# ScalarE's turn of an expert loop begun one split sooner, and fetched result rows added in eight operations of 512 columns

## The chip, the cores and the metric

The kernel runs on one core of a Trainium2 chip. The metric is the device time of one execution in microseconds. Five engines work side by side and wait for each other only through semaphores: TensorE (PE, matrix products into PSUM), VectorE (DVE), ScalarE (ACT), GpSimd (POOL) and SyncE (SP, which here issues the transfers).

## The reference

The kernel computes a two-layer encoder over 256 tokens of width 1024 in fp32. Layer 0 is Fourier mixing and a dense SwiGLU, layer 1 neighbourhood attention and a SwiGLU of 8 experts, of which each token takes two; a last RMSNorm closes it. The change lies in the experts:

```python
def moe_swiglu(h, w_router, b_router, w_gate, w_up, w_down):
    t = h.reshape(-1, D)                                  # 256 x 1024
    logits = t @ w_router + b_router                      # 8 experts
    top_val, top_idx = lax.top_k(logits, TOP_K)           # 2 of 8
    gates = jax.nn.softmax(top_val, axis=-1)
    ...
    def expert_block(args):                               # w_gate, w_up: 1024 x 3584
        xb, e = args                                      # w_down: 3584 x 1024
        return (jax.nn.silu(xb @ w_gate[e]) * (xb @ w_up[e])) @ w_down[e]
    ...
    out = jnp.zeros((T, D), h.dtype).at[tok_sorted].add(y * gate)
```

## The kernel before, in words

Products are done in fp32r, where one fp32 product takes three matmuls: each operand is split into a high part and a rest (the low part), and `three` (lines 1244 to 1250) adds high by high, high by low and low by high. All weights stream through the core once, in pieces of 128 x 2048 values (1 MB). For piece j there are three jobs: SP loads it into one of 7 buffers `raw`; ScalarE writes the high part (`split_hi`, line 454) into one of 3 buffers `w_hi`; VectorE writes the low part (`split_lo`, line 752) into one of 3 buffers `w_lo`; TensorE uses both with 12 matmuls of 512 columns. Since there are 3 buffers (`SPLIT = 3`), the split of piece j + 3 waits until TensorE has used piece j (`piece_used`).

An expert has 42 pieces, in the order of `EXPERT`: seven steps c of `gate c` (2 pieces), `up c` (2), and from step 1 on `down c-1` (2), and `down 6` at the end. After each gate ScalarE makes the silu (`silu`, line 672) and copies the transposed hidden values (line 678); after each up VectorE makes `hid` (line 1083).

Up to 128 tokens are given to each expert in a first sweep (experts 0 to 7); a second sweep for tokens beyond that is behind a test (`over`) and isn't entered with this input. Experts 0 to 6 are turns of a hardware loop on each engine (`Fori(0, LAST)`), expert 7 is written out behind it. TensorE does the first gate of the next expert (its pieces 0 and 1) at the end of its turn. ScalarE and VectorE run `AHEAD = SPLIT + 1 = 4` pieces ahead at the boundary: their turns skip j = 0 and end with the split of the next expert's piece 3. Inside a turn, at place j, the operations of that place come first and then the split of piece j + 3:

```python
for j, (kind, c, half) in enumerate(EXPERT):
    if j < AHEAD - SPLIT:
        continue
    if (kind, half) == ("gate", 1):
        silu(E, c)
...
    if ahead or j + SPLIT < PER_EXPERT:
        split_hi(j + SPLIT, E)
```

So ScalarE's turn begins with the silu of step 0, which waits until pieces 0 and 1 are used. The program builder sets an activation table load (ACT_TABLE_LOAD) in front of the first activation of a piece of program that needs another table than the one that may be in place; in the loop's body that is now the silu (line 672).

Results of experts 0 to 6 are written to a table in HBM (`results`), one row for each slot. While expert 7 runs, POOL fetches for each token its first and second row into `hn_hi` and `hn_lo` (line 435), and VectorE adds them to `h`, times the gates `g1` and `g2`, in `add_terms(0)` and `add_terms(1)`, which stand behind `hid` of steps 2 and 3 and ahead of the split of that place. `gate_weights` (six small operations) stands in step 1. Expert 7's own result is added at the end (`add_result`, line 1116).

Of the kernel before, what the change touches and what calls it, by code (L numbers as in the profile page):

```python
# [26 lines left out]
P = 128  # L27
D = 1024
S = 256
NB = S // P  # L30
# [11 lines left out]
BANK = 512  # L42
PIECE = 2048
RAW = 7
SPLIT = 3
# [64 lines left out]
PER_EXPERT = len(EXPERT)  # L110
assert PER_EXPERT % RAW == 0 and PER_EXPERT % SPLIT == 0

AHEAD = SPLIT + 1
# [12 lines left out]
def trunk(nc, x, norm_mix, norm_ffn, w_in, w_out, w_qkv, w_o, ffg, ffu, ffd, router_w, router_b,  # L126
          ewg, ewu, ewd, final_norm, gains_c, slide_c, dft_c, mask_c, ident_c, before_c, count_c, out):
    f32, f32r, bf16, i32, u32 = mybir.dt.float32, mybir.dt.float32r, mybir.dt.bfloat16, mybir.dt.int32, mybir.dt.uint32
    ALU, ACT, AX = mybir.AluOpType, mybir.ActivationFunctionType, mybir.AxisListType
# [22 lines left out]
    h = sb("h", [P, NB, D])  # L152
# [9 lines left out]
    half_power = sb("half_power", [P, NB])  # L162
# [37 lines left out]
             ("most", [P, 1], f32), ("flag", [P, 1], i32), ("rstd_of_slot", [P, 1], f32)]  # L200
    at_home("pad_arena")
    arena_start = nc.sbuf_base
    mo_more = [("y_row", [P, D], f32), ("place", [P, 2, NB], f32), ("past", [P, 2, NB], f32), ("source", [P, 2, NB], u32)]
    moe_l += mo_more
    sizes = [sum(width_of(shape) for _, shape, _ in l) for l in (fourier_l, attn_l, moe_l, bias_l + bias_l)]
    sb("arena", [P, max(sizes) // 4])
# [3 lines left out]
    fo, mo = (layout(l, arena_start) for l in (fourier_l, moe_l))  # L210
# [23 lines left out]
    def sem(name):  # L234
# [36 lines left out]
    y_act, y_dve, s_result, places_made, s_terms, terms_added, s_no_result = (sem(n) for n in (  # L271
        "y_act", "y_dve", "s_result", "places_made", "s_terms", "terms_added", "s_no_result"))
# [18 lines left out]
    SECOND = (NE, 2 * NE)  # L291
# [153 lines left out]
    def _(act):  # L445
        made = [0]

        def split_hi(j, E):
            s, w = slot_of(j, E, RAW), slot_of(j, E, SPLIT)
            rounds = 16 * (j // RAW + 1) if E is None else 16 * ((N0 + j) // RAW + 1) + E * (16 * PER_EXPERT // RAW)  # L450
            act.wait_ge(raw_in[s], rounds)
            if has_before(j, E, SPLIT):
                act.wait_ge(piece_used, piece(j, E, SPLIT))
            nc.scalar.activation(w_hi[w][:], raw[s][:], ACT.Copy).then_inc(hi_made, 1)  # L454
# [125 lines left out]
        n = at["down"][-1][-1]  # L580
# [112 lines left out]

        def expert(E, ahead, kept=True):

            for j, (kind, c, half) in enumerate(EXPERT):
                if j < AHEAD - SPLIT:
                    continue
                if (kind, half) == ("gate", 1):
                    silu(E, c)  # L700
                    if c:
                        hidden_hi(E, c - 1)
                if (kind, c, half) == ("down", STEPS - 2, 0):
                    if ahead:
                        gather_hi(E + 2)
                    hidden_hi(E, STEPS - 1)
                if (kind, c, half) == ("down", STEPS - 1, 1):
                    (result_hi if kept else result_copy)(E)
                if ahead or j + SPLIT < PER_EXPERT:
                    split_hi(j + SPLIT, E)  # L710
            if ahead:
                for j in range(PER_EXPERT + SPLIT, PER_EXPERT + AHEAD):
                    split_hi(j, E)

        gather_hi(1)
        assert made[0] == N1
        for j in range(SPLIT, AHEAD):
            split_hi(j, 0)
        with act.Fori(0, LAST) as E:
            expert(E, True, False)  # L720
        act.wait_ge(flag_done, 1)
# [2 lines left out]
        with act.If(over):  # L724
            act.wait_ge(e_gather, 2)
            act.wait_ge(hn_made, NB)
            act.wait_ge(terms_added, 2 * NB)
            for b in range(NB):
                nc.scalar.activation(mo["hn_hi"][:, b], hn[:, b], ACT.Copy).then_inc(hnr_hi, 1)
            gather_hi(NE + 1)  # L730
            for j in range(PER_EXPERT, PER_EXPERT + AHEAD):
                split_hi(j, LAST)
            with act.Fori(*SECOND) as E:
                expert(E, True)
            act.wait_ge(e_added, NB * (NE + 1))
        squares(4)

    @block.vector
    def _(dve):
# [108 lines left out]
        n = at["w_out"][0][-1]  # L848
# [24 lines left out]
        for c in range(DC):  # L873
# [5 lines left out]
            for b in range(NB):  # L879
                dve.wait_ge(d_silu, NB * c + b + 1)  # L880
                projected(dve, d_up, c, at["up"][c], b)
                if c:
                    dve.wait_ge(d_hidT, NB * (c - 1) + b + 1)
                nc.vector.scalar_tensor_tensor(out=hid[b][:, :w], in0=U[b][:, :w], scalar=rstd[:, 1, b:b + 1],
                                               in1=silu_g[b][:, :w], op0=ALU.mult, op1=ALU.mult).then_inc(d_hid, 1)
# [5 lines left out]
        n = at["down"][-1][-1]  # L891
# [52 lines left out]
        for p in range(PAIRS):  # L944
            for i in (2 * p, 2 * p + 1):
                dve.wait_ge(a_score, i + 1)
                if i >= 2:
                    dve.wait_ge(a_exp, NB * (i - 1))
                nc.vector.scalar_tensor_tensor(out=silu_g[i % 2][:].rearrange("p (n k) -> p n k", n=NB), in0=two(G[i % 2]),
                                               scalar=float(HD) ** -0.5, in1=head_bias(i), op0=ALU.mult, op1=ALU.add).then_inc(a_biased, 1)  # L950
# [41 lines left out]
        for b in range(NB):  # L992
            dve.wait_ge(sq_half, b + 1)
            half = h[:, b, BANK:]
            nc.vector.tensor_tensor_reduce(out=mo["xg"][:, BANK * b:BANK * (b + 1)], in0=half, in1=half, scale=1.0,
                                           scalar=mo["sumsq_half"][:, b:b + 1], op0=ALU.mult, op1=ALU.add,
# [13 lines left out]
        for b in range(NB):  # L1010
            nc.vector.scalar_tensor_tensor(out=mo["rest"][:, b], in0=G[b][:, NE:2 * NE], scalar=rstd[:, 3, b:b + 1],
                                           in1=mo["rb"][:], op0=ALU.mult, op1=ALU.add).then_inc(low_added, 1)
        for b in range(NB):
            dve.wait_ge(low_added, b + 1)
            link(nc.vector.scalar_tensor_tensor(out=mo["logit"][:, b], in0=G[b][:, 0:NE], scalar=rstd[:, 3, b:b + 1],
                                                in1=mo["rest"][:, b], op0=ALU.mult, op1=ALU.add))
        for n, (src, one) in enumerate((("logit", "first"), ("rest", "second"))):
# [6 lines left out]
            if n == 0:  # L1024
                link(nc.vector.scalar_tensor_tensor(out=mo["rest"][:], in0=mo["first"][:], scalar=-3e38,
                                                    in1=mo["logit"][:], op0=ALU.mult, op1=ALU.add))
# [11 lines left out]
        def gather_copy(E1):  # L1038

            for q in range(2):  # L1040
                cs = slice(BANK * q, BANK * (q + 1))
                dve.wait_ge(e_gather, 2 * by_products(E1) - 1 + q)
                if isinstance(E1, int) and E1 == 1:
                    made_copy = nc.vector.tensor_tensor(mo["xg"][:, cs], (G, U)[q][1][:], mo["gain"][:, 0, cs], ALU.mult)
                else:
                    made_copy = nc.vector.tensor_copy(mo["xg"][:, cs], (G, U)[q][1][:])
                made_copy.then_inc(e_xg[q], 1)
# [60 lines left out]

        def add_result(E, e):
            for b in range(NB):  # L1110
                dve.wait_ge(terms_added, NB + b + 1)
                for q in range(2):
                    dve.wait_ge(e_scatter, NB * (2 * (E - LAST) + q) + b + 1)
                    part = h[:, b, BANK * q:BANK * (q + 1)]
                    src = T[q] if b == 0 else (G, U)[q][1]
                    last = nc.vector.scalar_tensor_tensor(out=part, in0=src[:], scalar=mo["weight"][:, b, bass.ds(e, 1)],
                                                          in1=part, op0=ALU.mult, op1=ALU.add)
                last.then_inc(e_added, 1)
# [19 lines left out]
            link(nc.vector.tensor_tensor(mo["second"][:], mo["second"][:], each_token(mo["g2"][:]), ALU.mult))  # L1138
            link(nc.vector.tensor_tensor(mo["weight"][:], mo["first"][:], mo["second"][:], ALU.add))

        def add_terms(n):

            for b in range(NB):
                dve.wait_ge(s_terms, 16 * 2 * NB)
                if n:
                    dve.wait_ge(terms_added, b + 1)
                nc.vector.scalar_tensor_tensor(out=h[:, b], in0=mo[("hn_hi", "hn_lo")[n]][:, b].bitcast(f32),
                                               scalar=mo[("g1", "g2")[n]][:, b:b + 1], in1=h[:, b],
                                               op0=ALU.mult, op1=ALU.add).then_inc(terms_added, 1)

        def expert(E, sweep, ahead, kept=True):

            e = E - NE if sweep else E
# [3 lines that stand above are left out]
                if (kind, half) == ("gate", 1) and c:  # L1157
                    hidden_rest(E, c - 1)
                if (kind, c, half) == ("gate", 1, 1) and ahead and not sweep:
                    row_numbers(E)  # L1160
                if (kind, half) == ("up", 1):
                    hidden(E, c)
                    if c == 0 and kept:
                        next_selection(E, e, sweep, ahead)
                    elif c == 0:
                        dve.wait_ge(e_token, E)
                        select(sweep, e + 1)
                    if not kept or sweep:
                        pass
                    elif c == 1:  # L1170
                        gate_weights()
                    elif c == 2:
                        add_terms(0)
                    elif c == 3:
                        add_terms(1)
                    if c == STEPS - 1 and ahead and sweep:
                        gather_copy(E + 2)
                if (kind, c, half) == ("down", STEPS - 2, 0):
                    if ahead:
                        gather_lo(E + 2)  # L1180
                        rstd_is_one(E)
                    hidden_rest(E, STEPS - 1)
                if (kind, c, half) == ("down", STEPS - 1, 1):
                    (result_rest if kept else result_copy)(E)
                if ahead or j + SPLIT < PER_EXPERT:
                    split_lo(j + SPLIT, E)
            if ahead:
                for j in range(PER_EXPERT + SPLIT, PER_EXPERT + AHEAD):
                    split_lo(j, E)
            if kept:  # L1190
                add_result(E, e)
# [38 lines left out]
        for b in range(NB):  # L1230
            dve.wait_ge(fin_rstd, b + 1)
            for q in range(2):
                cs = slice(BANK * q, BANK * (q + 1))
# [594 lines left out]
```

## Time and profile before

| | |
|---|---|
| median of 3 runs | 1378.86 us (1378.75 to 1379.13) |
| the profiled execution: time | 1379.58 us |
| its span | 1377.8 us |
| TensorE busy | 1349.4 us (98%) |
| VectorE busy | 1111.5 us (81%) |
| ScalarE busy | 920.1 us (67%) |
| GpSimd busy | 33.8 us (2%) |
| granted TensorE clock, mean | 0.993 of full speed |

The span is the time from the first to the last instruction of the profiled execution; its time is a little longer. Busy time of an engine counts its own operations, not waits. In rows of a timeline the columns are: start in us from the span's start, duration in us, engine, line, operation, tile written <- tiles read, shape, count; then in brackets the idle time of the engine before it and what ended it. A count of x2 or x3 means operations merged into one row, whose duration runs from the first start to the last end. An engine's operations may overlap by about 0.1 us, since one begins before the last one's end is recorded. The duration of a matmul is modelled: matmuls start about every 0.23 us and are shown as 0.39 us long, so the starts say more than the durations.

### The profile page before, as it was taken

Reading aid. Unit: us, or ns where it says so; the run is one execution under the profiler, and the core shown is the slowest. Engines: PE = TensorE matmul, PEld = TensorE weight load, DVE = VectorE, ACT = ScalarE, POOL = GpSimd, SP = SyncE. Lnnn points to the kernel's source line nnn. Section 1 sums busy time; section 2 is a strip of 40 time slices with the busy share of each in tenths; the row PEclk is TensorE's granted clock in tenths of the full one; section 3 lists DMA queues with packets and bytes.
Section 4 is the critical chain, followed back from the end, with each engine's and each line's share of the span. In section 5 each row is a group of like instructions: output and inputs, shape, how many; then the busy total and the mean of one; then the engine's idle time right before and its main releaser. Section 6 shows DMA issues by size and latency. Waiting matters only on the chain.

```text
span 1377.8 us, 17441 instructions
## 1 busy us (share of the span) xinstructions
PE 1349.4 (98%) x6369; PEld 1120.4 (81%) x6369; DVE 1111.5 (81%) x811; ACT 920.1 (67%) x747; POOL 33.8 (2%) x48
## 2 busy tenths in 40 slices
PE   9999999999999999999999999999999999999997
PEld 7888888787877887888788788888878888888775
DVE  5756666655678888888988888898888889889987
ACT  6554444445647777777777777777777777777674
POOL 0000000000110000000000000000000000002000
PEclk9999999999989999999999999999999999999999
DMA  9666775462339999999999999999999999999992
GB/s 347 218 206 181 216 214 191 163 204 92 113 125 372 374 378 362 394 372 364 392 372 370 369 391 372 370 383 366 384 367 392 369 368 388 373 377 381 394 362 93
DMA packets 194940, 431.27 MB, mean 313 GB/s; under 512 B 19601, under 2 KB 22033, under 8 KB 194897
## 3 DMA queue, kind: packets, MB, share of 16 engines
q1 hardware_dynamic: 178752, 415.66, 82.8%
q0 software_dynamic: 3360, 11.78, 2.2%
q10 hardware_dynamic: 12784, 3.26, 1.7%
q8 instruction: 27, 0.44, 0.1%
q14 instruction: 17, 0.13, 0.0%
HBM read 424.89 MB, written 5.78 MB: 313 GB/s over the span
## 4 chain that ended last, share of the span: by engine, by line
PE 89%; DVE 5%; ACT 3%; issue 2%; DMA 0%; ACTq 0%; POOL 0%; DVEq 0%
PE bank_G L1248 10%; PE bank_G L1250 10%; PE bank_G L1249 10%; PE bank_U L1248 9%; PE bank_U L1250 9%; PE bank_U L1249 9%; PE bank_Y L1248 8%; PE bank_Y L1250 8%; PE bank_Y L1249 8%; DVE w_lo L752 2%; PE bank_T L1689 2%; ACT w_hi L454 1%; PE bank_T L1248 1%; PE bank_T L1250 1%; PE bank_T L1249 1%
## 5 line engine op out<-in xcount | busy, mean ns | idle before, releaser
L752 DVE TENSOR_TENSOR w_lo<-raw,w_hi 128x2048 fp32r<-128x2048 f32 x390 | 885.8, 2289 | 195.2 <-ACT w_hi L454 195.1
L454 ACT ACTIVATE w_hi<-raw 128x2048 fp32r<-128x2048 f32 x390 | 747.0, 1919 | 286.7 <-PE bank_U L1250 91.1
L1248 PE MATMUL bank_Y<-w_hi,hidT_hi 128*128 128x512 f32 x492 | 192.3, 391 | 0.0
L1250 PE MATMUL bank_Y<-w_hi,hidT_lo 128*128 128x512 f32 x492 | 191.6, 390 | 0.0
L1249 PE MATMUL bank_Y<-w_lo,hidT_hi 128*128 128x512 f32 x492 | 191.5, 389 | 0.0
L1248 PE MATMUL bank_G<-w_hi,xg_hi 128*128 128x512 f32 x448 | 175.6, 392 | 11.0 <-DVE w_lo L752 10.0
L1248 PE MATMUL bank_U<-w_hi,xg_hi 128*128 128x512 f32 x448 | 179.1, 400 | 0.0
L1250 PE MATMUL bank_U<-w_hi,xg_lo 128*128 128x512 f32 x448 | 175.0, 391 | 0.0
L1250 PE MATMUL bank_G<-w_hi,xg_lo 128*128 128x512 f32 x448 | 174.5, 390 | 0.0
L1249 PE MATMUL bank_U<-w_lo,xg_hi 128*128 128x512 f32 x448 | 174.5, 390 | 0.0
L1249 PE MATMUL bank_G<-w_lo,xg_hi 128*128 128x512 f32 x448 | 174.4, 389 | 0.0
L1248 PEld LDWEIGHTS bank_G<-w_hi,xg_hi 128*128 128x128 f32 x448 | 84.1, 188 | 32.5 <-DVE w_lo L752 9.3
L1250 PEld LDWEIGHTS bank_Y<-w_hi,hidT_lo 128*128 128x128 f32 x492 | 92.3, 188 | 19.3
L1248 PEld LDWEIGHTS bank_Y<-w_hi,hidT_hi 128*128 128x128 f32 x492 | 92.3, 188 | 19.3
L1249 PEld LDWEIGHTS bank_Y<-w_lo,hidT_hi 128*128 128x128 f32 x492 | 92.4, 188 | 18.8
L1250 PEld LDWEIGHTS bank_U<-w_hi,xg_lo 128*128 128x128 f32 x448 | 84.1, 188 | 18.3
L1250 PEld LDWEIGHTS bank_G<-w_hi,xg_lo 128*128 128x128 f32 x448 | 84.1, 188 | 17.6
L1249 PEld LDWEIGHTS bank_G<-w_lo,xg_hi 128*128 128x128 f32 x448 | 84.1, 188 | 17.1
L1249 PEld LDWEIGHTS bank_U<-w_lo,xg_hi 128*128 128x128 f32 x448 | 84.3, 188 | 16.2
L1248 PEld LDWEIGHTS bank_U<-w_hi,xg_hi 128*128 128x128 f32 x448 | 84.2, 188 | 15.9
L1248 PE MATMUL bank_G<-w_hi,act_hi 128*128 128x512 f32 (+1 forms) x176 | 67.6, 384 | 2.2 <-DVE act_lo L777 1.4
L1248 PE MATMUL bank_U<-w_hi,act_hi 128*128 128x512 f32 (+1 forms) x176 | 67.6, 384 | 0.3 <-DVE act_lo L773 0.3
(302 smaller groups left out, 1366.6 us busy)
## 6 DMA issues: line engine op xcount, KB each, us to landing
raw<-in_expert_w_gate SPq DMA_DIRECT2D x112, 1024.0 KB, 7.4
raw<-in_expert_w_up SPq DMA_DIRECT2D x112, 1024.0 KB, 7.5
raw<-in_expert_w_down SPq DMA_DIRECT2D x112, 1024.0 KB, 7.4
raw<-in_nat_w_qkv SPq DMA_DIRECT2D x12, 1024.0 KB, 5.1
raw<-in_ffn_w_gate SPq DMA_DIRECT2D x11, 1024.0 KB, 8.9
raw<-in_ffn_w_up SPq DMA_DIRECT2D x11, 1024.0 KB, 6.0
raw<-in_ffn_w_down SPq DMA_DIRECT2D x11, 1024.0 KB, 5.1
raw<-in_fourier_w_out SPq DMA_DIRECT2D x4, 1024.0 KB, 15.9
```

Source lines behind the costliest of these rows:

```text
L454: nc.scalar.activation(w_hi[w][:], raw[s][:], ACT.Copy).then_inc(hi_made, 1)
L752: nc.vector.tensor_tensor(w_lo[w][:], raw[s][:], w_hi[w][:].bitcast(f32), ALU.subtract).then_inc(lo_made, 1)
L1248: nc.tensor.matmul(out_, xh, wh, start=start, stop=False)
L1249: nc.tensor.matmul(out_, xh, wl, start=False, stop=False)
L1250: return nc.tensor.matmul(out_, xl, wh, start=False, stop=stop)
L1689: last = nc.tensor.transpose(T[c % 2][:, P * k:P * (k + 1)], hid[c % 2][:, P * k:P * (k + 1)], ident[:])
```

## The change

ScalarE's turn now begins at j = 0, with the split of piece 3, and ends with the split of piece 2 of the next expert; what stood before the loop for piece 3 goes. In front of each turn stands a silu of one column of `half_power` (a constant) into a new one-column tile, which nobody reads. VectorE's and SP's turns stay as they are. `add_terms(n)`, two operations of 1024 columns for each n, becomes `add_term(n, b, q)`, one operation of 512 columns; eight of them stand in steps 2 to 5 of expert 7, one behind `hid` (q = 0) and one ahead of the split of the first down piece (q = 1) of each step. The count that `add_result` and the second sweep wait for becomes 4 x NB = 8.

```diff
-... ("source", [P, 2, NB], u32)]
+... ("source", [P, 2, NB], u32), ("silu_first", [P, 1], f32)]
@@ ScalarE
         def expert(E, ahead, kept=True):
 
+            nc.scalar.activation(mo["silu_first"][:], half_power[:, 0:1], ACT.Silu)
             for j, (kind, c, half) in enumerate(EXPERT):
-                if j < AHEAD - SPLIT:
-                    continue
                 if (kind, half) == ("gate", 1):
                     silu(E, c)
...
                 if ahead or j + SPLIT < PER_EXPERT:
                     split_hi(j + SPLIT, E)
-            if ahead:
-                for j in range(PER_EXPERT + SPLIT, PER_EXPERT + AHEAD):
-                    split_hi(j, E)
 
         gather_hi(1)
         assert made[0] == N1
-        for j in range(SPLIT, AHEAD):
-            split_hi(j, 0)
         with act.Fori(0, LAST) as E:
             expert(E, True, False)
@@ VectorE
         def add_result(E, e):
             for b in range(NB):
-                dve.wait_ge(terms_added, NB + b + 1)
+                dve.wait_ge(terms_added, 4 * NB)
...
-        def add_terms(n):
-
-            for b in range(NB):
-                dve.wait_ge(s_terms, 16 * 2 * NB)
-                if n:
-                    dve.wait_ge(terms_added, b + 1)
-                nc.vector.scalar_tensor_tensor(out=h[:, b], in0=mo[("hn_hi", "hn_lo")[n]][:, b].bitcast(f32),
-                                               scalar=mo[("g1", "g2")[n]][:, b:b + 1], in1=h[:, b],
-                                               op0=ALU.mult, op1=ALU.add).then_inc(terms_added, 1)
+        def add_term(n, b, q):
+
+            cs = slice(BANK * q, BANK * (q + 1))
+            dve.wait_ge(s_terms, 16 * 2 * NB)
+            if n:
+                dve.wait_ge(terms_added, 2 * b + q + 1)
+            nc.vector.scalar_tensor_tensor(out=h[:, b, cs], in0=mo[("hn_hi", "hn_lo")[n]][:, b, cs].bitcast(f32),
+                                           scalar=mo[("g1", "g2")[n]][:, b:b + 1], in1=h[:, b, cs],
+                                           op0=ALU.mult, op1=ALU.add).then_inc(terms_added, 1)
...
-                    elif c == 2:
-                        add_terms(0)
-                    elif c == 3:
-                        add_terms(1)
+                    elif 2 <= c < 6:
+                        add_term((c - 2) // 2, c % 2, 0)
...
+                if (kind, half) == ("down", 0) and kept and not sweep and 1 <= c < 5:
+                    add_term((c - 1) // 2, (c - 1) % 2, 1)
```

## Rows read from the trace of the kernel before

**Rows 1.** The page's chain that ended last, by engine.
```profile
PE 89%; DVE 5%; ACT 3%; issue 2%; DMA 0%; ACTq 0%; POOL 0%; DVEq 0%
```

**Rows 2.** Waits of TensorE, 410 to 1250 us, then 1250 to 1378: total, times, longest.
```profile
PE bank_G L1248 <- DVE w_lo L752: 6.4, 7, 0.9
...
PE bank_G L1248 <- DVE w_lo L752: 3.6, 3, 1.6
```

**Rows 3.** Timeline of ScalarE at one boundary; last, all table loads of line 672.
```profile
525.05 1.93 ACT L454 ACTIVATE w_hi<-raw 128x2048 fp32r<-128x2048 f32 x1 [0.31 <-PE bank_Y L1250]
527.77 1.93 ACT L454 ACTIVATE w_hi<-raw 128x2048 fp32r<-128x2048 f32 x1 [0.80 <-PE bank_G L1250]
530.63 1.28 ACT L672 ACT_TABLE_LOAD   x1 [0.93 <-PE bank_G L1250]
531.92 0.69 ACT L672 ACTIVATE silu_g<-bank_G,rstd_of_slot 128x512 f32<-128x512 f32 x1
532.51 5.51 ACT L454 ACTIVATE w_hi<-raw 128x2048 fp32r<-128x2048 f32 x3
...
L672 ACT ACT_TABLE_LOAD x7: 1283/1283/1283, 410.7 to 1130.3; - x7
```

**Rows 4.** Timeline of VectorE at the same boundary.
```profile
529.73 2.29 DVE L752 TENSOR_TENSOR w_lo<-raw,w_hi 128x2048 fp32r<-128x2048 f32 x1 [0.35 <-ACT w_hi L454]
534.45 4.49 DVE L752 TENSOR_TENSOR w_lo<-raw,w_hi 128x2048 fp32r<-128x2048 f32 x2 [2.43 <-ACT w_hi L454]
```

**Rows 5.** Timeline of TensorE at the same boundary.
```profile
530.06 0.39 PE L1250 MATMUL bank_G<-w_hi,xg_lo 128*128 128x512 f32 x1
...
535.50 0.39 PE L1250 MATMUL bank_U<-w_hi,xg_lo 128*128 128x512 f32 x1
536.79 0.50 PE L1248 MATMUL bank_G<-w_hi,xg_hi 128*128 128x512 f32 x1 [0.90 <-DVE w_lo L752]
...
537.61 0.40 PE L1248 MATMUL bank_G<-w_hi,xg_hi 128*128 128x512 f32 x1
```

**Rows 6.** Timeline of ScalarE at the last boundary, behind the loop.
```profile
1247.28 1.92 ACT L454 ACTIVATE w_hi<-raw 128x2048 fp32r<-128x2048 f32 x1 [0.80 <-PE bank_G L1250]
1250.00 0.69 ACT L672 ACTIVATE silu_g<-bank_G,rstd_of_slot 128x512 f32<-128x512 f32 x1 [0.80 <-PE bank_G L1250]
```

**Rows 7.** Timeline of ScalarE in the dense layer and at the kernel's start.
```profile
79.59 1.92 ACT L454 ACTIVATE w_hi<-raw 128x2048 fp32r<-128x2048 f32 x1 [1.12 <-POOL rstd L398]
81.53 1.28 ACT L572 ACT_TABLE_LOAD   x1
82.82 1.27 ACT L572 ACTIVATE silu_g<-bank_G,rstd 128x512 f32<-128x512 f32 x2
...
3.47 0.20 ACT L506 ACTIVATE silu_g<-half_power 128x2 f32<-128x2 f32 x1
```

**Rows 8.** Timeline of VectorE in the last expert, steps 2 and 4.
```profile
1286.08 0.74 DVE L1083 SCALAR_TENSOR_TENSOR hid<-bank_U,rstd_of_slot,silu_g 128x512 f32<-128x512 f32 x1
1286.74 2.47 DVE L1147 SCALAR_TENSOR_TENSOR h<-hn_hi,g,h 128x1024 f32<-128x1024 f32 x2
1289.13 6.69 DVE L752 TENSOR_TENSOR w_lo<-raw,w_hi 128x2048 fp32r<-128x2048 f32 x3
...
1324.04 2.28 DVE L752 TENSOR_TENSOR w_lo<-raw,w_hi 128x2048 fp32r<-128x2048 f32 x1
1326.60 2.29 DVE L752 TENSOR_TENSOR w_lo<-raw,w_hi 128x2048 fp32r<-128x2048 f32 x1 [0.28 <-ACT w_hi L454]
```

**Rows 9.** Timeline of TensorE in the last expert, steps 2 and 4.
```profile
1289.59 0.39 PE L1250 MATMUL bank_Y<-w_hi,hidT_lo 128*128 128x512 f32 x1
1291.57 0.47 PE L1248 MATMUL bank_G<-w_hi,xg_hi 128*128 128x512 f32 x1 [1.59 <-DVE w_lo L752]
...
1292.33 0.39 PE L1248 MATMUL bank_G<-w_hi,xg_hi 128*128 128x512 f32 x1
...
1327.11 0.39 PE L1248 MATMUL bank_G<-w_hi,xg_hi 128*128 128x512 f32 x1
```

More of the change, by code:

```diff
@@ L202, in trunk @@
     arena_start = nc.sbuf_base
-    mo_more = [("y_row", [P, D], f32), ("place", [P, 2, NB], f32), ("past", [P, 2, NB], f32), ("source", [P, 2, NB], u32)]
+    mo_more = [("y_row", [P, D], f32), ("place", [P, 2, NB], f32), ("past", [P, 2, NB], f32), ("source", [P, 2, NB], u32), ("silu_first", [P, 1], f32)]
     moe_l += mo_more
@@ L726, in _ @@
             act.wait_ge(hn_made, NB)
-            act.wait_ge(terms_added, 2 * NB)
+            act.wait_ge(terms_added, 4 * NB)
             for b in range(NB):
@@ L730, in _ @@
             gather_hi(NE + 1)
-            for j in range(PER_EXPERT, PER_EXPERT + AHEAD):
+            for j in range(PER_EXPERT, PER_EXPERT + SPLIT):
                 split_hi(j, LAST)
@@ L734, in _ @@
                 expert(E, True)
+            split_hi(PER_EXPERT + SPLIT, SECOND[1] - 1)
             act.wait_ge(e_added, NB * (NE + 1))
```

## The prediction

> **What bounds the kernel now.** I read the page's chain first: nine tenths of it is TensorE [rows 1], so only an edit that takes away time in which TensorE stands still, or adds some, can move the end. The views of waits say where it stands still while the experts run. In the loop over experts 0 to 6 there are seven waits, all for a low part (`w_lo`) that VectorE makes, and in the last expert three, up to 1.6 us long [rows 2]. The reader should then go to the timelines of one boundary between experts and of the last expert, since the change edits just these two places.
>
> At the boundary, TensorE finishes the second gate piece of the new expert (piece 1) at U = 530.06 + 0.39 = 530.45. It goes on with pieces 2 and 3 without a gap, and stands before piece 4: 535.50 to 537.61 is 2.11 us for four starts that take 4 x 0.227 elsewhere ((535.50 - 530.06) / 24 = 0.227), so 1.20 us are lost [rows 5]. Why is piece 4 late? ScalarE had piece 3's high part done at 527.77 + 1.92 = 529.69, waited for U, and only then loaded its activation table (1.28 us), made the silu, and began piece 4's high part at 532.51 [rows 3]. VectorE took that up at 534.45 after 2.43 us of idleness [rows 4], ended at 534.45 + 2.29 = 536.74, and TensorE started at 536.79. The table load happens seven times, once at the head of each turn [rows 3]. The eighth boundary, where the loop has ended, has no table load: the silu begins 0.80 us after the split before it [rows 6], and no wait of TensorE stands there. Seven boundaries lose 7 x 1.20 = 8.4 us.
>
> In the last expert the two long stalls come from `add_terms`. Two 1024-column additions hold VectorE for 1289.13 - 1286.74 = 2.39 us ahead of a low part [rows 8]; it ends at 1289.13 + 2.29 = 1291.42, and TensorE goes on at 1291.57. From 1289.59 to 1292.33 are 2.74 us for four starts, so 2.74 - 0.91 = 1.83 us lost [rows 9]. The three waits have 3.6 us with 1.6 as the longest [rows 2], so two of that size, together 3.66 us lost; the third, 3.6 - 2 x 1.6 = 0.4 us, follows `gate_weights` and isn't touched.
>
> **The turn of ScalarE.** The edit removes no work from the turn; it puts the loop's head one split sooner and a one-column silu in front, so the table load belongs to that silu, which waits for no semaphore. New order: split of piece 2, loop branch, table load, one-column silu, split of piece 3, (wait for U) silu, split of piece 4. SP's and POOL's queues and VectorE's order stay; no DMA is moved.
>
> Step by step, in the times of this boundary. The split of piece 2 ends at 525.05 + 1.92 = 526.97. A table load that waits for nothing starts 0.02 us after the operation before it and the next silu follows at once: 79.59 + 1.92 = 81.51, then 81.53, then 82.82 [rows 7]. So: load at 526.99, one-column silu at 528.28. The nearest row for it is a two-column copy of 0.20 us [rows 7], and one operation may begin 0.10 before the last one's end (531.92 + 0.69 against 532.51 [rows 3]), so the split of piece 3 begins between 528.38 and 528.48. I take 528.43, 0.66 later than now (527.77).
>
> Does that hurt? Its high part ends at 530.35, 0.10 before U, so the silu starts right after U. The low part of piece 3 moves from 529.73 to 530.39 and ends at 532.68. Piece 3's first slot on TensorE is at 535.73 - 12 x 0.227 = 533.01. A low part must be ready some time before its slot: the one that ended at 536.74 cost 1.20 us, so for the slot at 535.73 the latest harmless end is 535.54, 0.19 ahead. For piece 3 that is 532.82; now it ends at 532.02. Slack left 0.14 us: it fits, barely.
>
> And piece 4: silu at U + 0.04 = 530.49 in place of 531.92, so all behind it is 1.43 us earlier; the low part ends at 536.74 - 1.43 = 535.31, before 535.54. Slack 0.23 us, and the stall goes: -1.20 us, seven times, **-8.4 us**. At the first boundary the load falls into the idleness before piece 0 is used up; at the eighth the one-column silu (0.1 to 0.2 us) fits into the 0.80 us of idleness [rows 6]. Cover that costs nothing now: if the split of piece 3 came later than 528.43 by more than 0.14 us, each further us is a us lost per boundary, up to the 1.2 gained.
>
> The branch itself has no row. It was hidden so far: it lay between the issue of the split at 527.77 and U, at most 2.68 us. Now only the split of piece 2 (1.92 us) covers it, so from 0 to 0.76 us of it can be exposed. I take 0: the first boundary has no branch back, yet the seven waits come to 6.4 us with 0.9 as the longest [rows 2], so it waits as long as the others.
>
> A switch of tables could cost more than its load. The row has 81.51 to 82.82, 1.31 us, for a complete switch with work on both sides [rows 7], and the sum goes by that. The Trainium skill, "ScalarE: Activation LUTs", section "What ACT_TABLE_LOAD costs", puts a switch at the load and a drain beside it, about 2.66 us together. That speaks against the change: by the row the boundary gains 1.20, by the page next to nothing (the rival of the drain, below). The trace doesn't agree with the page here.
>
> **The fetched rows.** Four 1024-column additions become eight of 512 columns. A 1024-column one takes 1.20 us in sequence (2.39 / 2). A 512-column one has no row: below it is half, 0.60; above, if the price went by the instruction, 1.20. VectorE's three-operand operation on 512 columns (`hid`, the same form, one input in PSUM) takes 0.66 in sequence: it starts at 1286.08, the next operation at 1286.74 [rows 8]. I take 0.66. VectorE's work grows by 8 x 0.66 - 4 x 1.20 = 0.5 us; what counts is where it stands.
>
> In an undisturbed step the low part of the next gate's first piece runs 1324.04 to 1326.33 [rows 8] and its slot is 1327.11 [rows 9]. From the stall, the margin ahead of a slot is 1291.42 against 1289.82 (the slot) + 1.83: an end of 1289.59 is harmless, so 0.23. Slack: 1327.11 - 0.23 - 1326.33 = 0.55 us (check: 2.39 - 0.55 = 1.84 lost, as measured). One addition of 0.66 gives 0.11 us lost. The next low part (1326.60, ending 1328.89, slot 1329.83) has slack 0.71. In the changed kernel it starts at 1324.70 + 2.21 (a low part in sequence) + 0.66 (the second addition) = 1327.57, ends at 1329.86, and may end at 1329.60 + 0.11 already lost: 0.15 more. Low parts follow each other at 2.21 and pieces at 12 x 0.227 = 2.72, so VectorE regains 0.5 us with each of the next pieces, and nothing is carried into the next step. Four steps (c = 2 to 5) lose 4 x 0.26 = 1.0 us in place of 3.66: **-2.6 us**. With 0.60 per addition it is 4 x 0.14 = 0.6, so -3.1; with 1.20 it is 4 x (0.65 + 0.69) = 5.4, so +1.7. The rows were fetched by then: the first addition follows `hid` without idleness [rows 8], so the waits in front of the additions pass. `add_result` waits for eight in place of four, long done.
>
> **Sum.** -8.4 - 2.6 = -11.0 us. The profiled execution has a span of 1377.8 and a time of 1379.58, 1.8 around it; changed, the span is 1366.8. The median of the runs is 1378.86, 0.7 below the profiled time; I take the difference off the median: **1367.9 us**.
>
> **Rivals.**
> *The branch back is exposed.* Then the split of piece 3 is later than now by 0.66 + 0.76 = 1.42, and its low part ends at 532.02 + 1.42 = 533.44 against 532.82: 0.62 lost. The silu then waits for ScalarE (531.11), low part 4 ends at 535.93, within 535.54 + 0.62: no more. The six boundaries behind a branch give 6 x 0.62 = 3.7 back: 1371.6. For it: nothing shows the branch alone. Against: TensorE's own branch at 530.3 leaves no gap. Chance 0.12. The Trainium skill ("Runtime: NRT & Kernel Launch", section "Instruction fetch mechanics") says that a taken branch whose target has left the instruction window waits for a fetch; no row here shows such a wait.
>
> *The engine drains at a switch.* If a switch cost as much again as its load (1.28 us more), the split of piece 3 would be 1.94 us later than now, its low part would end at 533.96 and 1.14 be lost, against 1.20 now: 6 x 0.06 = 0.4 gained, with the first boundary's 1.2 (its load is under cover) and the additions' 2.6 together 4.2: 1374.7. Against: the 1.31 us of [rows 7]. Chance 0.04. With the drain of the Trainium skill's page named above, 1.24 us would be lost at each of the six, and the time be 1375.3.
>
> *The additions are dear.* At 1.20 each the second part costs 1.7 in place of giving 2.6: 1372.2. Against: the row of `hid`. Chance 0.05.
>
> *Slower.* The branch back has no cover at all: ScalarE takes it only when the split of piece 2 has ended. Its whole length is bounded by 2.68 us, from the issue of the split at 527.77 to U [rows 3, 5]. Split of piece 3 later by 0.66 + 2.68 = 3.34, less the 0.80 that its low part has now (532.82 - 532.02): 2.54 lost, 1.34 more than now, over six boundaries +8.0, less 1.2 (the first) and 2.6: +4.2, 1383.1. It decides from some 2.0 us exposed. Against: a branch taken only behind a split had 0.76 us in the trace (529.69 to U), not 2.68. Chance 0.02.
>
> *The change does nothing at the boundary:* a load stays before the waited silu, or another wait lies just behind (a transfer of weights). Then only -2.6: 1376.3. Against: in the seven boundaries ScalarE is released by TensorE [rows 3], and the two lists of TensorE's waits name no transfer [rows 2]; the one-column silu is the body's first operation. Chance 0.05.
>
> **How the numbers follow.** My forecast has 0.72, with its own range from 1366.3 (additions at 0.60 take 0.5 us off 1367.9, no loss from them at all another 0.6, and half a us for what the steps round) to 1369.8 (0.3 us left at each of six boundaries). The range 1366.2 to 1372.0 takes in the exposed branch and leaves out the four last rivals, 0.16. About 0.2% (2.8 us) is what a measurement of this kernel can tell from no change. Faster by more: 0.72 + 0.12 + 0.04 + 0.05 = 0.93; within: no effect at the boundary, 0.05; slower: 0.02.
>
> **What would show it.** In the changed trace: the table load about 0.02 us behind the split of piece 2 and at no other place; the split of piece 3 some 0.66 us later relative to U; the silu 0.04 us after U; the seven waits of TensorE gone from the loop; silus of one boundary to the next 118.7 us apart in place of 119.9. In the last expert the waits of 1.6 us gone and up to eight of 0.1 to 0.2 us in their place, in steps 2 to 5; an addition of about 0.74 us. The prediction is wrong if the load isn't followed at once by the one-column silu, if the split of piece 3 starts over 0.8 us late, or if a wait for piece 3 appears on TensorE.

## The result

The changed kernel takes 1367.91 us (median of 4 runs, 1367.32 to 1367.96) against 1378.80 us (4 runs, 1378.04 to 1379.13) for the kernel before. The ratio is 0.9921 with an interval from 0.9904 to 0.9938: faster by 10.9 us, where 11.0 were forecast. The span of the profiled execution went from 1377.8 to 1366.0 us, 11.8 less, of which 0.6 lie ahead of the experts: TensorE ends the first gate of expert 0 at 410.54 before and at 409.97 now. From there to the end it is 967.2 against 956.0 us, 11.2 less.

### The profile page after: what moved, and what is told of

Read it like the earlier page. It is cut to its first block, busy times and chain, and to the rows that moved or that the text cites. A ratio compares the mean times of both kernels' runs of the same rounds, so it can differ in the third digit from the quotient of the medians.

```text
span 1366.0 us, 17462 instructions
## 1 busy us (share of the span) xinstructions
PE 1347.7 (99%) x6369; PEld 1120.3 (82%) x6369; DVE 1111.9 (81%) x815; ACT 922.8 (68%) x755; POOL 33.3 (2%) x48
## 4 chain that ended last, share of the span: by engine, by line
PE 93%; DVE 3%; ACT 1%; DMA 1%; SPq 1%; issue 1%; POOL 0%; DVEq 0%; ACTq 0%
PE bank_G L1243 10%; PE bank_G L1245 10%; PE bank_G L1244 10%; PE bank_U L1243 10%; PE bank_U L1245 10%; PE bank_U L1244 10%; PE bank_Y L1243 8%; PE bank_Y L1245 8%; PE bank_Y L1244 8%; PE bank_T L1684 2%; DMA raw<-in_fourier_w_out 1%; PE bank_T L1243 1%; PE bank_T L1245 1%; PE bank_T L1244 1%; DVE w_lo L747 1%
```

## The profile after

In the page, the parts that answer to [rows 1] and to the busy line: TensorE works 1347.7 us (1349.4 before), of a span 11.8 shorter, and the chain has 93% TensorE in place of 89%.

```profile
PE 1347.7 (99%) x6369; PEld 1120.3 (82%) x6369; DVE 1111.9 (81%) x815; ACT 922.8 (68%) x755; POOL 33.3 (2%) x48
...
PE 93%; DVE 3%; ACT 1%; DMA 1%; SPq 1%; issue 1%; POOL 0%; DVEq 0%; ACTq 0%
```

The waits of TensorE, 405 to 1245 us, are an empty list now. From 1240 us to the end one of the three of [rows 2] is left, that of `gate_weights`:

```profile
PE bank_G L1243 <- DVE w_lo L747: 0.4, 1, 0.4
```

ScalarE at the boundary of [rows 3] (columns as there):

```profile
523.31 1.92 ACT L454 ACTIVATE w_hi<-raw 128x2048 fp32r<-128x2048 f32 x1 [0.32 <-PE bank_Y L1245]
525.25 1.28 ACT L696 ACT_TABLE_LOAD   x1
526.54 0.20 ACT L696 ACTIVATE silu_first<-half_power 128x1 f32<-128x1 f32 x1
526.65 1.90 ACT L454 ACTIVATE w_hi<-raw 128x2048 fp32r<-128x2048 f32 x1
528.91 0.69 ACT L672 ACTIVATE silu_g<-bank_G,rstd_of_slot 128x512 f32<-128x512 f32 x1 [0.35 <-PE bank_G L1245]
```

The split of piece 2 ends at 523.31 + 1.92 = 525.23; the load starts 0.02 us later, branch included. The one-column silu takes 0.20 us and holds the next operation 0.11.

VectorE at the same boundary, the rows that answer to [rows 4]:

```profile
528.59 2.29 DVE L747 TENSOR_TENSOR w_lo<-raw,w_hi 128x2048 fp32r<-128x2048 f32 x1 [0.96 <-ACT w_hi L454]
531.43 4.49 DVE L747 TENSOR_TENSOR w_lo<-raw,w_hi 128x2048 fp32r<-128x2048 f32 x2 [0.55 <-ACT w_hi L454]
```

And TensorE, the rows that answer to [rows 5]: end of piece 1, first start of piece 2, last start of piece 3, first of piece 4.

```profile
528.33 0.39 PE L1245 MATMUL bank_G<-w_hi,xg_lo 128*128 128x512 f32 x1
528.55 0.39 PE L1243 MATMUL bank_U<-w_hi,xg_hi 128*128 128x512 f32 x1
...
533.76 0.40 PE L1245 MATMUL bank_U<-w_hi,xg_lo 128*128 128x512 f32 x1
534.00 0.40 PE L1243 MATMUL bank_G<-w_hi,xg_hi 128*128 128x512 f32 x1
```

U is 528.33 + 0.39 = 528.72 here. Between 533.76 and 534.00 are 0.24 us, a plain spacing, where 1.29 stood before [rows 5]. VectorE's idleness ahead of piece 4 has gone from 2.43 to 0.55.

In the last expert, VectorE in step 2, for [rows 8]:

```profile
1277.16 0.74 DVE L1078 SCALAR_TENSOR_TENSOR hid<-bank_U,rstd_of_slot,silu_g 128x512 f32<-128x512 f32 x1
1277.82 0.74 DVE L1142 SCALAR_TENSOR_TENSOR h<-hn_hi,g,h 128x512 f32<-128x512 f32 x1
1278.48 2.28 DVE L747 TENSOR_TENSOR w_lo<-raw,w_hi 128x2048 fp32r<-128x2048 f32 x1
1280.68 0.75 DVE L1142 SCALAR_TENSOR_TENSOR h<-hn_hi,g,h 128x512 f32<-128x512 f32 x1
1281.35 6.87 DVE L747 TENSOR_TENSOR w_lo<-raw,w_hi 128x2048 fp32r<-128x2048 f32 x3
...
1294.18 0.74 DVE L1078 SCALAR_TENSOR_TENSOR hid<-bank_U,rstd_of_slot,silu_g 128x512 f32<-128x512 f32 x1
```

An addition of 512 columns holds VectorE for 1278.48 - 1277.82 = 0.66 us. The step lasts 1294.18 - 1277.16 = 17.02 us. An undisturbed one lasted 16.80 before (`hid` at 1323.38 and 1340.18), so 0.22 us are lost. All four steps with additions, from `hid` at 1277.16 to `hid` at 1345.20, last 68.04 us, 0.84 more than four undisturbed ones.

## The experiments

Ten kernels, told in the order of the questions. A turn is the distance of two boundaries' silus (line 672) in ScalarE's timeline, from the second boundary to the seventh, by five. The last column is the time from U of the first boundary (where TensorE ends piece 1 of expert 0) to the end of the profiled execution. Both are finer measures than the time, since they leave out everything ahead of the experts, where the profiled executions of these kernels differ by up to 2.2 us in code that they share (U between 408.3 and 410.5). They are read from one execution each. The intervals of the ratios are 2.5 to 4.7 us wide, so kernels that lie 1 or 2 us apart can't be told apart by their times alone.

| kernel | time, us | ratio to before, interval | turn, us | first U to the end, us |
|---|---|---|---|---|
| before | 1378.8 | | 119.93 | 967.2 |
| changed | 1367.91 | 0.9904 to 0.9938 | 118.72 | 956.0 |
| turn_only | 1370.54 | 0.9926 to 0.9953 | 118.73 | 958.9 |
| terms_only | 1375.80 | 0.9968 to 0.9986 | 119.96 | 964.5 |
| no_silu | 1375.35 | 0.9964 to 0.9984 | 119.90 | 964.2 |
| silu_before_loop | 1370.51 | 0.9927 to 0.9954 | 118.72 | 959.2 |
| silu_in_front | 1372.48 | 0.9948 to 0.9975 | 119.05 | 961.6 |
| silu_512 | 1368.79 | 0.9916 to 0.9948 | 118.92 | 957.1 |
| silu_1024 | 1371.46 | 0.9935 to 0.9966 | 119.38 | 960.0 |
| one_1024_each_step | 1369.21 | 0.9918 to 0.9946 | 118.73 | 958.0 |
| additions_at_down | 1365.74 | 0.9891 to 0.9922 | 118.74 | 954.5 |
| load_before_loop_and_down | 1367.00 | 0.9899 to 0.9926 | 118.76 | 955.1 |

The turn of the kernel before is that of its seven table loads, (1130.3 - 410.7) / 6 [rows 3]. The kernel before was run again beside each group of kernels (medians 1378.57 to 1378.87 us), and each ratio is taken to its own.

**Each part alone.** `turn_only` has the changed ScalarE and the old `add_terms`; `terms_only` the old ScalarE and the eight additions.

> Only ScalarE's turn is changed; the additions are the four of 1024 columns as before. If the two parts are independent and the table load is the whole of the seven stalls, TensorE loses 1.20 us less at each of seven boundaries: 8.4 us less than before, 1370.4 us, with the two waits of 1.6 us still in the last expert. The rival, that the additions and the turn help each other (a lighter VectorE at the boundary), would leave it above 1371.5.

> Only the additions are changed; ScalarE's turn is as before. Steps 2 to 5 of the last expert are then each 17.01 us as in the changed kernel, 0.21 longer than an undisturbed one of 16.80, in place of two that lose 1.83: 3.66 - 0.85 = 2.8 us less than before, 1376.0 us, and the seven waits of 0.9 us stay. The rival, that the additions give nothing and the turn gives all of the 10.9 us, has 1378.8.

-8.3 us and -3.1 us against 1378.87 (the runs of the kernel before beside them), together -11.4 where both give -10.9. By the last column it is -8.3, -2.7 and -11.2. TensorE's waits, `turn_only` in the last expert, then `terms_only` in the loop:

```profile
PE bank_G L1243 <- DVE w_lo L747: 3.6, 3, 1.6
```
```profile
PE bank_G L1248 <- DVE w_lo L752: 6.4, 7, 0.9
```

Each part takes away its own waits and leaves the other's untouched; they are independent to 0.2 us, and the rivals of both expectations fall.

**Is it the sooner turn or the place of the load?** `no_silu` is the changed kernel without the new silu:

```diff
         def expert(E, ahead, kept=True):
-            nc.scalar.activation(mo["silu_first"][:], half_power[:, 0:1], ACT.Silu)
             for j, (kind, c, half) in enumerate(EXPERT):
```

> The changed kernel without the one-column silu: the turn begins one split sooner, but the program builder now sets two table loads into each turn, one in front of the split of piece 3 and one in front of the real silu, which waits for the gate. Theory (what counts is that no table load lies behind the wait for the gate): the first load is under cover (the split of piece 3 is 0.5 us later, within 0.8 of slack), the second costs what it cost before, 1.20 us at each of seven boundaries: 1367.9 + 8.4 = 1376.3 us. Rival (the sooner turn itself is what helps): 1367.9 to 1369 us.

1375.35 us, 7.4 above the changed kernel (8.4 expected): the time of `terms_only`. In the last column it is 8.2 above, and a turn is 1.18 longer, so 0.8 of the missing 1.0 lies outside the experts and isn't a smaller stall. ScalarE at its boundary:

```profile
524.78 1.28 ACT L454 ACT_TABLE_LOAD   x1
526.08 1.92 ACT L454 ACTIVATE w_hi<-raw 128x2048 fp32r<-128x2048 f32 x1
528.42 1.28 ACT L672 ACT_TABLE_LOAD   x1 [0.42 <-PE bank_G L1244]
529.72 0.69 ACT L672 ACTIVATE silu_g<-bank_G,rstd_of_slot 128x512 f32<-128x512 f32 x1
```

There are two loads now, since the copy of the split comes first in the body and is given a load of its own. The first costs nothing (the turn is that of `terms_only` to 0.06 us); the second stands behind the wait for the gate, and all seven waits are back (6.3 us in total). The sooner turn by itself gives nothing.

**And the load without the sooner turn?** `silu_before_loop` is the kernel before with one line, ahead of the loop and not in it:

```diff
+        nc.scalar.activation(mo["silu_first"][:], half_power[:, 0:1], ACT.Silu)
         with act.Fori(0, LAST) as E:
             expert(E, True, False)
```

> The kernel before with one single one-column silu ahead of the loop and nothing else changed (turns of ScalarE as before, old additions). The program builder then sets one table load ahead of the loop and none in it. If the load alone made the stalls, each boundary looks like the eighth of the kernel before, TensorE doesn't wait there, and the time is 8.4 us less than before: 1370.4 us, the same as with ScalarE's turn changed alone. Rival (the late start of the turn, at the wait for the gate, costs something by itself): between 1371 and 1378.

1370.51 us and a turn of 118.72, where `turn_only` has 1370.54 and 118.73. Both ways into the loop's body now leave the same table in place, and the builder sets no load into it. The boundary, without a load:

```profile
522.68 1.92 ACT L454 ACTIVATE w_hi<-raw 128x2048 fp32r<-128x2048 f32 x1 [0.32 <-PE bank_Y L1251]
525.40 1.92 ACT L454 ACTIVATE w_hi<-raw 128x2048 fp32r<-128x2048 f32 x1 [0.80 <-PE bank_G L1251]
528.27 0.69 ACT L672 ACTIVATE silu_g<-bank_G,rstd_of_slot 128x512 f32<-128x512 f32 x1 [0.96 <-PE bank_G L1251]
```

So the load behind the wait is the cause of the stall in the turns, and the late start of the turn costs nothing. The first boundary is an exception that the expectation didn't see. The one load stands behind the split of piece 3, the small silu behind it, and the real silu starts 0.73 us behind U (409.58 against 408.46 + 0.39). TensorE's first start of piece 4 is then 0.53 us behind the last of piece 3 (413.90 to 414.43) in place of 0.23. By the last column this kernel is 0.3 us behind `turn_only`.

**A load half under cover.** `silu_in_front` puts the one-column silu in front of the old turn, behind the split of piece 3:

```diff
         def expert(E, ahead, kept=True):
+            nc.scalar.activation(mo["silu_first"][:], half_power[:, 0:1], ACT.Silu)
             for j, (kind, c, half) in enumerate(EXPERT):
                 if j < AHEAD - SPLIT:
                     continue
```

> The kernel before with the one-column silu in front of each turn, the turn itself still begun with the wait for the gate. The table load (1.28 us) then starts when the split of piece 3 has ended (0.76 us before U), not at U: it ends 0.52 behind U, the small silu takes 0.10 to 0.20, the real silu starts 0.65 to 0.7 behind U in place of 1.47, so the split of piece 4 is 0.82 earlier and 0.38 of the 1.20 us is left at each of seven boundaries: 1378.8 - 5.7 = 1373.1 us. Rival (the load isn't started before the real silu is free to go): 1378.8 us.

1372.48 us; the turn of 119.05 leaves 119.05 - 118.72 = 0.33 us of stall (0.38 expected). The load starts when the split ends, and its last half microsecond sticks out past U, which is TensorE's start at 527.33 + 0.39 = 527.72:

```profile
525.03 1.92 ACT L454 ACTIVATE w_hi<-raw 128x2048 fp32r<-128x2048 f32 x1 [0.80 <-PE bank_G L1251]
526.97 1.28 ACT L696 ACT_TABLE_LOAD   x1
528.26 0.20 ACT L696 ACTIVATE silu_first<-half_power 128x1 f32<-128x1 f32 x1
528.37 0.67 ACT L672 ACTIVATE silu_g<-bank_G,rstd_of_slot 128x512 f32<-128x512 f32 x1
```

**How thin is the slack of piece 3?** The prediction had 0.14 us. Two kernels delay the split of piece 3 by a known amount, with a wider first silu (512 columns as fp32; 1024 as bf16 in the same room):

```diff
-            nc.scalar.activation(mo["silu_first"][:], half_power[:, 0:1], ACT.Silu)
+            nc.scalar.activation(mo["silu_first"][:], half_power[:, 0:1].to_broadcast([P, 512]), ACT.Silu)
```

> The changed kernel with the first silu 512 columns wide in place of one (its input is the same constant read again and again). It takes about 0.63 us in place of 0.20, so the split of piece 3 is 0.43 us later. From the changed kernel's trace the low part of piece 3 ends at 530.88 and its slot is at 531.27, with 0.19 of margin ahead of it: slack 0.20 us. So 0.23 lost at each of six boundaries (at the first the silu is under cover), 1.4 us: 1369.3 us, with six short waits of TensorE for piece 3. Rival (the slack isn't that thin, VectorE or the three buffers carry more): 1367.9 us.

> The changed kernel with the first silu 1024 columns wide (written as bf16, which halves the room and not the time): about 1.06 us in place of 0.20, the split of piece 3 0.86 us later. Beyond the slack of 0.20 that is 0.66 at each of six boundaries, 4.0 us: 1371.9 us. The real silu is then late as well, by 0.5 us, but piece 4 has by then as much more time as piece 3 has lost, so it doesn't add. If it added, 1374 to 1375. Rival (slack not thin): 1367.9 to 1369.

The silus take 0.63 and 1.05 us and the turns are 118.92 and 119.38: 0.20 and 0.66 lost, where 0.23 and 0.66 were expected. The times are 0.9 and 3.6 above the changed kernel's (1.4 and 4.0 expected); by the last column it is 1.1 and 4.0. At 512 columns the list of TensorE's waits is empty, where six short ones were expected; the loss shows in the starts at piece 3 alone (530.17, 530.48, 530.82, so 0.31 and 0.34 apart in place of 0.23). At 1024 columns TensorE waits six times, and for `bank_U`, that is for piece 3, no longer for piece 4:

```profile
PE bank_U L1246 <- DVE w_lo L750: 2.1, 6, 0.4
```

The delay of 0.86 beyond a slack of 0.20 is lost one for one, and the late silu doesn't add to it. The first boundary isn't among the six, since there the load and the silu lie in front of the first gate.

**Size or number of the additions?** `one_1024_each_step` leaves the four additions whole and puts one in each step:

```diff
                     elif 2 <= c < 6:
-                        add_term((c - 2) // 2, c % 2, 0)
+                        add_term((c - 2) // 2, c % 2)
...
-                if (kind, half) == ("down", 0) and kept and not sweep and 1 <= c < 5:
-                    add_term((c - 1) // 2, (c - 1) % 2, 1)
```

> The changed kernel's turn, and the four additions of 1024 columns left whole, but one in each of the steps 2 to 5, behind hid. VectorE is held 1.20 us against 0.55 of slack: 0.65 lost in each of four steps, 2.6 us, against 0.21 x 4 = 0.85 in the changed kernel and 3.66 with two in a step: 1369.7 us. Rival (what helps is the size of the operation, not how many stand in a step): 1370.7 us, as with the turn alone.

1369.21 us (1369.7 expected), and four waits of 0.39 us where two additions at once cost 1.6; the fifth of the list is that of `gate_weights`. The list, then VectorE:

```profile
PE bank_G L1240 <- DVE w_lo L747: 2.0, 5, 0.4
...
1277.18 0.74 DVE L1078 SCALAR_TENSOR_TENSOR hid<-bank_U,rstd_of_slot,silu_g 128x512 f32<-128x512 f32 x1
1277.84 1.27 DVE L1141 SCALAR_TENSOR_TENSOR h<-hn_hi,g,h 128x1024 f32<-128x1024 f32 x1
1279.03 6.69 DVE L747 TENSOR_TENSOR w_lo<-raw,w_hi 128x2048 fp32r<-128x2048 f32 x3
...
1294.66 0.75 DVE L1078 SCALAR_TENSOR_TENSOR hid<-bank_U,rstd_of_slot,silu_g 128x512 f32<-128x512 f32 x1
```

The step is 1294.66 - 1277.18 = 17.48 us, 0.68 lost, 2.7 in four steps. So each step has one allowance of 0.55 us behind `hid`, and what counts is how often it is used. Spreading over four steps brings about 1.0 of the 2.8 us. The other 1.8 come from halving the operations and putting the second halves one place later; which of the two it is was not tried apart.

**A better place.** `additions_at_down` moves both additions of a step one place on, to the first and the second down piece, and puts the halves of `gate_weights` at the down pieces of step 1:

```diff
-                    elif c == 1:
-                        gate_weights()
-                    elif 2 <= c < 6:
-                        add_term((c - 2) // 2, c % 2, 0)
...
-                if (kind, half) == ("down", 0) and kept and not sweep and 1 <= c < 5:
-                    add_term((c - 1) // 2, (c - 1) % 2, 1)
+                if kind == "down" and kept and not sweep and c == 0:
+                    gate_weights(half)
+                if kind == "down" and kept and not sweep and 1 <= c < 5:
+                    add_term((c - 1) // 2, (c - 1) % 2, half)
```

> The changed kernel with the same eight additions of 512 columns moved: none behind hid, one ahead of the split at each of the two down places of steps 2 to 5, and gate_weights' six small operations in two threes at the down places of step 1. At the first down place VectorE has 0.28 us of idleness and 0.71 of slack behind it, at the second 0.42 more: 0.66 fits at each, so TensorE doesn't wait in the last expert at all. The residue of 4 x 0.21 and the 0.66 us of step 1 go: 1367.9 - 1.5 = 1366.4 us. Rival (the residue comes from the sum of VectorE's work in a step, not from its place): 1367.9 us or just 0.6 below.

1365.74 us, the shortest time of all (its interval overlaps that of the changed kernel; the last column has 1.5 us less, as expected), and the list of TensorE's waits is empty from 405 us to the end. VectorE does the same work in the same step, so the residue of the changed kernel came from the place:

```profile
1274.96 0.74 DVE L1078 SCALAR_TENSOR_TENSOR hid<-bank_U,rstd_of_slot,silu_g 128x512 f32<-128x512 f32 x1
1275.62 2.28 DVE L747 TENSOR_TENSOR w_lo<-raw,w_hi 128x2048 fp32r<-128x2048 f32 x1
1277.82 0.75 DVE L1144 SCALAR_TENSOR_TENSOR h<-hn_hi,g,h 128x512 f32<-128x512 f32 x1
...
1291.77 0.75 DVE L1078 SCALAR_TENSOR_TENSOR hid<-bank_U,rstd_of_slot,silu_g 128x512 f32<-128x512 f32 x1
```

1291.77 - 1274.96 = 16.81 us: an undisturbed step.

**Both, with the load out of the loop.** `load_before_loop_and_down` joins `silu_before_loop` and these places.

> The kernel before with the single one-column silu ahead of the loop (no table load in it, ScalarE's turns as before) and the additions at the two down places. If both parts are independent this is the same time as the run with the changed turn and the additions at the down places, 1366.4 us; were the thin slack of 0.20 us at the boundary in the changed kernel still costing something, this one would be faster by that, up to 0.5 us.

1367.00 us, 1.3 above the run just told, which neither outcome of the expectation allows. The views of line 672, silus from first to last, of `additions_at_down` and then of this kernel:

```profile
L672 ACT ACTIVATE silu_g<-bank_G,rstd_of_slot x56: 688/689/696, 408.6 to 1334.8; 128x512 f32<-128x512 f32 x56
```
```profile
L672 ACT ACTIVATE silu_g<-bank_G,rstd_of_slot x56: 677/689/692, 410.9 to 1337.1; 128x512 f32<-128x512 f32 x56
```

Both are 926.2 us from the first silu to the last, but that hides a difference, since in this kernel the first silu is itself late, as in `silu_before_loop`. ScalarE and TensorE at its first boundary:

```profile
409.55 1.28 ACT L719 ACT_TABLE_LOAD   x1
410.84 0.20 ACT L719 ACTIVATE silu_first<-half_power 128x1 f32<-128x1 f32 x1
410.95 0.68 ACT L672 ACTIVATE silu_g<-bank_G,rstd_of_slot 128x512 f32<-128x512 f32 x1
...
409.85 0.39 PE L1249 MATMUL bank_G<-w_hi,xg_lo 128*128 128x512 f32 x1
...
415.29 0.39 PE L1249 MATMUL bank_U<-w_hi,xg_lo 128*128 128x512 f32 x1
415.80 0.50 PE L1247 MATMUL bank_G<-w_hi,xg_hi 128*128 128x512 f32 x1
```

U is 409.85 + 0.39 = 410.24, and the silu starts 0.71 behind it, against 0.20 in `additions_at_down` (408.62, U at 408.03 + 0.39 = 408.42). Piece 4 starts 0.51 behind the last start of piece 3 in place of 0.23. From U to the end this kernel takes 955.1 us against 954.5, 0.6 more. The rest of the difference of the profiled executions (spans 1365.3 and 1362.9) lies ahead of U, 1.8 us, in code that the two kernels share. Stage by stage (start:end, length, each engine's busy time, granted clock, DMA), the same two kernels just ahead of the loop:

```profile
380.00:405.00 25.00, 21.35 (x120) 18.57 (x119) 19.14 (x51) 12.36 (x23) 1.80 (x3) 0.86 0.26 89
```
```profile
380.00:405.00 25.00, 21.73 (x116) 18.68 (x115) 18.02 (x51) 11.54 (x21) 1.80 (x3) 0.80 0.28 101
```

The clock granted there, in the router's stage, was 0.86 and 0.80 of full speed, and the changed kernel had 0.73. In the first layer the second of these two profiles is 0.8 us later already. Whether such differences go with the kernels or only with the executions wasn't tested. So of the 1.3 us, 0.4 to 0.6 come from the place of the one load (0.4 in the two starts at piece 4, 415.29 to 415.80 and on to 416.14, and 0.6 in the whole stretch), and the rest stays open. The gain of `additions_at_down` over the changed kernel in the experts is 927.6 (410.2 to 1337.8) - 926.2 = 1.4 us, where 1.5 were expected; in these two the first silu stands alike, 0.20 behind U.

## Why the prediction was right

*The seven stalls.* Right in cause and size. A turn became 1.21 us shorter, seven of them 8.5 us (8.4 forecast), and `turn_only` moved by 8.3. That the sum of 11.0 met 10.9 to 0.1 us is in part luck: the four executions of the kernel before alone differ by 1.1 us (1378.04 to 1379.13). The trace, from U of the first boundary to the end, has 11.2.

*The load follows at once, and the branch is under cover.* Right: 0.02 us behind the split. The forecast took 0 of the 0.76 us that might have been exposed, and 0.02 is what both together leave. The reason given for 0 couldn't decide it, though: in the kernel before, the branch lay under a split and an idle stretch of 0.76 us, so a branch of any length up to 2.68 us would have left the waits of all seven boundaries alike. The 0 was a guess that came out right. The rivals of the exposed branch and of the branch without cover fall. The rule of the Trainium skill ("Runtime: NRT & Kernel Launch", section "Instruction fetch mechanics") on a taken branch whose target has left the instruction window names a wait that doesn't show here; that the head of this loop had left the window isn't shown either.

*No drain.* Right: from the load at 525.25 to the small silu at 526.54 are 1.29 us, and before it 0.02. The 2.66 us of the Trainium skill ("ScalarE: Activation LUTs", section "What ACT_TABLE_LOAD costs") are not seen at this boundary; the trace bears out the row of [rows 7].

*Split of piece 3.* It starts 2.07 us ahead of U; forecast 530.45 - 528.43 = 2.02. Its slack was forecast at 0.14 and is 0.20 by the trace, and the probes with 512 and 1024 columns confirm it.

*The silu at U + 0.04* was off: it starts at 528.91, 0.19 behind U. The forecast took the figure of the eighth boundary [rows 6], though the load in [rows 3] already started 0.18 behind U (530.63 against 530.45). The first silu of each turn is 0.15 later than that of the eighth boundary, with or without a load in the turn (`silu_before_loop` is idle for 0.96 us where the eighth boundary is for 0.80); the other six silus of a turn start 0.04 behind their gate, as those of the last expert do. So piece 4's low part ends at 531.43 + 2.29 = 533.72 against a limit of 534.00 - 0.19 = 533.81: slack 0.09 in place of 0.23. The stalls agree: before, the silu was 1.28 us later than this and 1.20 were lost; in `silu_in_front` it was 0.46 later (528.37 - 527.72 = 0.65 behind U) and 0.33 were lost, so 0.08 and 0.13 were free. This is the thinnest place of the change, thinner than piece 3. It was enough, and the number had no effect on the time.

*The additions.* 0.66 us each in sequence, as taken from `hid`. The loss per step is 0.21, forecast 0.26; four steps 0.84 (1.0). Before, the two disturbed steps lasted 18.65 us each, 3.7 lost together, so the second part gives 2.8 to 2.9 us (2.6), and `terms_only` moved by 3.1. The small waits forecast in steps 2 to 5 don't appear in the list of waits; the loss is read from the length of the steps.

*Not foreseen* was that half of the edit isn't needed: the prediction called the one-column silu and the sooner turn one mechanism. One silu ahead of the loop does the same in the turns without touching any order, and with more slack for piece 3. Placed behind the split of piece 3 it leaves 0.3 to 0.6 us at the first boundary; ahead of that split it would have been under cover by the rows (in `silu_before_loop` ScalarE is idle for 3.36 us ahead of it), but no run shows it.

## What to carry to other kernels

Look in a hardware loop for work that the builder sets in front of an operation on its own account, such as a table load: if it stands behind a wait, it is on the path in each turn, however small its share. Give it an operation that waits for nothing, or make both ways into the loop's body agree so that it isn't needed, and then look where the one load that is left stands. And small work for an engine that feeds the bottleneck should be put where that engine has idleness next to it: each step has an allowance (by the rows 0.55 us here behind `hid` and 0.7 one place later, where 0.66 fitted without a wait), and only what goes beyond it costs.

## What the runs showed of the hardware

- A table load on a busy ScalarE costs 1.29 to 1.30 us from its start to the next operation and 0.02 ahead of it, no more, also right behind a loop's branch (525.23 to 526.54).
- Where the program builder puts the load decides what it costs: none of it under cover (`no_silu`, the first of two loads), 0.33 us with its last half microsecond exposed (`silu_in_front`), 1.2 us behind the wait (the kernel before).
- A silu whose input is one constant read 512 or 1024 times takes 0.63 us (512, written as fp32) and 1.05 us (1024, written as bf16) against 0.20 for one column.
- The first silu of a turn in the loop started 0.19 us behind the matmul that it waits for. The other six of the turn and all seven of the last expert, in straight code, started 0.04 behind theirs. What makes the 0.15 us wasn't tried.
